# mLSTM stage of a two-layer streaming encoder: scores and the keys' transposes in one matmul per head, values transposed ahead of them

## The reference

```
def step(carry, xs):
    C, n, m = carry
    qc, kc, vc, ic, fc = xs
    b = jnp.cumsum(fc, axis=-1)
    D = b[..., :, None] - b[..., None, :] + ic[..., None, :]
    D = jnp.where(causal, D, NEG)
    inter = b + m[..., None]
    mt = jnp.maximum(inter, jnp.max(D, axis=-1))
    S = jnp.einsum('bhtd,bhsd->bhts', qc, kc) * jnp.exp(D - mt[..., None])
    w_inter = jnp.exp(inter - mt)
    num = jnp.einsum('bhts,bhsd->bhtd', S, vc) + w_inter[..., None] * jnp.einsum('bhvk,bhtk->bhtv', C, qc)
    den = jnp.sum(S, axis=-1) + w_inter * jnp.einsum('bhk,bhtk->bht', n, qc)
    h = num / jnp.maximum(jnp.abs(den), jnp.exp(-mt))[..., None]
    mL = mt[..., -1]
    ws = jnp.exp(b[..., -1:] - b + ic - mL[..., None])
    decay = jnp.exp(b[..., -1] + m - mL)
    C_new = decay[..., None, None] * C + jnp.einsum('bhs,bhsv,bhsk->bhvk', ws, vc, kc)
```

## Time and profile before

| | us |
|---|---|
| median of three timed runs | 1317.18 |
| lowest, highest | 1316.38, 1317.22 |
| the profiled execution, its own time | 1317.47 |
| its span, first to last instruction | 1315.7 |
| TensorE busy | 1296.2 |
| VectorE busy | 897.3 |
| ScalarE busy | 611.2 |
| mLSTM stage of layer 0, own keys of pair 0 to own keys of pair 3 | 29.10 |

### The profile page before, as it was taken

One profiled execution on the slowest core, in us unless ns is written; L12 is line 12 of the kernel. 1 busy time (PEld: TensorE's weight loads), 2 busy tenths in 40 slices (PEclk: granted clock), 3 DMA queues, 4 the chain that ended last, 5 costly groups with the idle time before them and its releaser, 6 DMA issues.

```text
span 1315.7 us, 24594 instructions
## 1 busy us (share of the span) xinstructions
PE 1296.2 (99%) x9943; PEld 1264.8 (96%) x9943; DVE 897.3 (68%) x1504; ACT 611.2 (46%) x1134; POOL 62.6 (5%) x43
## 2 busy tenths in 40 slices
PE   7999999999999999999999999999999999999998
PEld 6999899999999999999999998999999999999997
DVE  7776787798586475586666768878965846846734
ACT  6324335488256155165242333456852732822833
POOL 0000001000000000000610000000000000000032
PEclk9999999999999999999999999999999999999999
DMA  7322220223232232222252222212322322322312
GB/s 220 82 71 66 64 65 33 81 72 121 65 97 97 66 94 96 90 69 96 84 123 71 65 65 65 65 33 81 97 97 65 97 97 65 114 77 74 119 65 73
DMA packets 115630, 109.74 MB, mean 83 GB/s; under 512 B 18830, under 2 KB 109398, under 8 KB 115542
## 3 DMA queue, kind: packets, MB, share of 16 engines
q1 hardware_dynamic: 110256, 104.54, 26.3%
q10 hardware_dynamic: 5286, 3.97, 1.0%
HBM read 104.69 MB, written 3.81 MB: 82 GB/s over the span
## 4 chain that ended last, share of the span: by engine, by line
PE 89%; DVE 6%; ACT 3%; issue 1%; DMA 0%; SPq 0%; ACTq 0%; DVEq 0%
PE psum L1717 56%; PE psum L2039 8%; PE psum L2041 8%; PE psum L2040 8%; PE psum L1770 1%; PE psum L1859 1%; PE psum L1955 1%; PE psum L1947 1%; PE psum L1920 1%; PE psum L1936 1%; PE psum L1964 1%; ACT w_hi L545 1%; PE psum L1892 1%; PE psum L1888 1%; PE psum L1877 0%
## 5 line engine op out<-in xcount | busy, mean ns | idle before, releaser
L1717 PE MATMUL psum<-hid_h,w_hi 128*128 128x288 f32 x1232 | 266.6, 297 | 0.0
L1717 PE MATMUL psum<-hid_l,w_hi 128*128 128x288 f32 x1232 | 263.8, 295 | 0.0
L1717 PE MATMUL psum<-hid_h,w_lo 128*128 128x288 f32 x1232 | 263.7, 295 | 0.0
L1717 PEld LDWEIGHTS psum<-hid_h,w_hi 128*128 128x128 f32 x1232 | 197.3, 188 | 1.1 <-issue 0.3
L1717 PEld LDWEIGHTS psum<-hid_h,w_lo 128*128 128x128 f32 x1232 | 197.6, 188 | 0.0
L1717 PEld LDWEIGHTS psum<-hid_l,w_hi 128*128 128x128 f32 x1232 | 197.4, 188 | 0.0
L1717 PE MATMUL psum<-xh,w_hi 128*128 128x288 f32 x800 | 178.9, 305 | 2.8 <-ACT x L590 1.9
L1602 DVE TENSOR_TENSOR tmp<-psum,rms 128x576 f32<-128x576 f32 x63 | 47.7, 758 | 185.9 <-PE psum L1717 185.8
L1717 PE MATMUL psum<-xh,w_lo 128*128 128x288 f32 x800 | 172.1, 296 | 0.0
L1717 PE MATMUL psum<-xl,w_hi 128*128 128x288 f32 x800 | 172.0, 296 | 0.0
L803 ACT ACTIVATE w_hi<-stage 128x1024 fp32r<-128x1024 f32 x64 | 67.7, 1058 | 219.0 <-PE psum L1717 218.2
(11 more groups left out here) (331 smaller groups left out, 2546.8 us busy)
## 6 DMA issues: line engine op xcount, KB each, us to landing
stage<-in_w_up SPq DMA_DIRECT2D x32, 1024.0 KB, 5.6
stage<-in_w_down SPq DMA_DIRECT2D x32, 1024.0 KB, 5.1
stage<-in_w_in SPq DMA_DIRECT2D x18, 1024.0 KB, 5.2
stage<-in_w_in SPq DMA_DIRECT2D x16, 256.0 KB, 4.4
stage<-in_w_out SPq DMA_DIRECT2D x8, 512.0 KB, 6.9
stage<-in_w_out SPq DMA_DIRECT2D x4, 1024.0 KB, 5.7
z<-in_x_prompt SPq DMA_DIRECT2D x4, 512.0 KB, 5.6
out<-z SPq DMA_DIRECT2D x3, 512.0 KB, 2.7
```

The lines of the kernel that those rows point to most:

```text
L1717: ins = M(acc[t % 2][:, a, :], lhs(w), mov[:, k, a * HALF:(a + 1) * HALF], start=first and n == 0, stop=last and n == 2)
```

## The change

The keys are the stationary side of the scores' product already (`z[:, h, cs]`). The change makes the moving side 256 columns wide: the identity and the queries, in two blocks of 128. The identity's block gives the keys' transpose, the queries' block the scores. So that one access pattern reaches both, `z` gets 128 columns ahead of its first tile, which GpSimd fills with the identity once. The results of heads 0 and 1 go to bank 4 and those of heads 2 and 3 to bank 7; the values' transposes go to bank 6 and stand ahead of the scores. The units are dealt out anew. The short pair's merged product also moves 256 columns, of which 64 queries are used.

```diff
-M_FILL = ((2, 1, 1, 1), (2, 2, 1, 1), (2, 2, 1, 1), (2, 2, 1, 1), (2, 1, 0, 0))
+M_FILL = ((1, 1, 3), (2, 1, 3), (2, 1, 3), (2, 1, 3), (2, 1, 0))
...
-        z = place("z", [P, 4 * MH, T])
+        z_all = place("z", [P, P + 4 * MH * T])
+        z = z_all[:, P:].rearrange("p (n t) -> p n t", n=4 * MH)
...
+            pool.wait_ge(s_const, 16)
+            nc.gpsimd.tensor_copy(z_all[:, 0:P], ident).then_inc(s_idc, 1)
             pool.wait_ge(s_rcon, 1)
...
                 def values(p):
                     r = rows(p)
                     act.wait_ge(s_tv, NP * l + p + 1)
-                    A(vtok[0:r, :, 0:MD], psum[0:r, 7, :].rearrange("p (h d) -> p h d", h=MH), ACT.Copy).then_inc(s_vev, 1)
+                    A(vtok[0:r, :, 0:MD], psum[0:r, 6, :].rearrange("p (h d) -> p h d", h=MH), ACT.Copy).then_inc(s_vev, 1)
...
                     r = rows(p)
-                    act.wait_ge(s_tk, NP * l + p + 1)
+                    act.wait_ge(s_sw, NP * l + p + 1)
                     act.wait_ge(s_gtd, l + 1)
                     for h in range(MH):
-                        ins = A(ktok[0:r, h], psum[0:r, 7, h * MD:(h + 1) * MD], ACT.Copy, scale=gT[0:r, p, 0, h:h + 1])
+                        keys_out = psum[0:r, (4, 7)[h // 2], h % 2 * 256:h % 2 * 256 + P]
+                        ins = A(ktok[0:r, h], keys_out, ACT.Copy, scale=gT[0:r, p, 0, h:h + 1])
                     ins.then_inc(s_kev, 1)
...
                     fill("m", p, 0)
-                    head_squares(p)
                     if p < NP - 1:
                         values(p + 1)
+                    head_squares(p)
                     fill("m", p, 1)
...
-                    V.tensor_tensor(sw[0:r, :, 0:r], ch(4, p)[0:r], eexp[0:r, :, 0:r], ALU.mult).then_inc(s_sw, 1)
+                    pairs = lambda buf: buf[0:r].rearrange("p (k h) t -> p k h t", k=2)[:, :, :, 0:r]
+                    scores = psum[0:r, 4:8:3, :].rearrange("p k (h b t) -> p k h b t", h=2, b=2)[:, :, :, 1, 0:r]
+                    V.tensor_tensor(pairs(sw), scores, pairs(eexp), ALU.mult).then_inc(s_sw, 1)
...
                     r, cs = rows(p), pair_cols(p)
                     if p:
                         pe.wait_ge(s_st, NP * l + p)
+                        pe.wait_ge(s_hx, MH * (NP * l + p))
                     for h in range(MH):
-                        ins = M(psum[0:r, 4, head(p, h)], z[:, h, cs], z[:, 4 + h, cs], start=True, stop=True)
+                        at = P + (4 + h) * T + p * P
+                        ident_and_query = z_all[:, 0:2 * at].rearrange("p (b c) -> p b c", b=2)[:, :, 0:P]
+                        out = psum[0:r, (4, 7)[h // 2], h % 2 * 256:(h % 2 + 1) * 256].rearrange("p (b c) -> p b c", b=2)
+                        ins = M(out, z[:, h, cs], ident_and_query, start=True, stop=True)
                     ins.then_inc(s_swp, 1)
...
-                        ins = TR(psum[0:r, 7, h * MD:(h + 1) * MD], z[:, tile + h, pair_cols(p)], ident)
-                    ins.then_inc(signal, 1)
+                        ins = TR(psum[0:r, 6, h * MD:(h + 1) * MD], z[:, 8 + h, pair_cols(p)], ident)
+                    ins.then_inc(s_tv, 1)
...
                 scores(0)
                 exponents(0)
-                token_major(0, 0, s_tk)
                 fill(l, "a", NC, 0)
                 fill(l, "p", 0, 0)
-                pe.wait_ge(s_kev, NP * l + 1)
+                pe.wait_ge(s_ao, NC * (l + 1))
                 pe.wait_ge(s_evac, TILES * l + S_WOA)
-                token_major(0, 8, s_tv)
+                values(0)
                 fill(l, "p", 0, 1)
-                pe.wait_ge(s_ao, NC * (l + 1))
...
                     if p:
                         from_state(p)
+                    if p < NP - 1:
+                        if p:
+                            pe.wait_ge(s_ownc, (NP - 1) * l + p)
+                        else:
+                            pe.wait_ge(s_hx, MH * (a + 1))
+                        values(p + 1)
                     fill(l, "m", p, 1)
                     if p < NP - 1:
                         scores(p + 1)
-                        pe.wait_ge(s_hx, MH * (a + 1))
-                        token_major(p + 1, 8, s_tv)
                         exponents(p + 1)
                     fill(l, "m", p, 2)
-                    if p < NP - 1:
-                        pe.wait_ge(s_vev, a + 2)
-                        token_major(p + 1, 0, s_tk)
-                    fill(l, "m", p, 3)
```

More of the change, by code:

```diff
@@ L269, in hymba_step @@
         s_aoh, s_ao = sem("s_aoh"), sem("s_ao")
-        s_tv, s_vev, s_tk, s_kev = sem("s_tv"), sem("s_vev"), sem("s_tk"), sem("s_kev")
+        s_tv, s_vev, s_kev = sem("s_tv"), sem("s_vev"), sem("s_kev")
         s_e, s_ex, s_swp, s_sw = sem("s_e"), sem("s_ex"), sem("s_swp"), sem("s_sw")
@@ L277, in hymba_step @@
         s_zclear = sem("s_zclear")
+        s_idc = sem("s_idc")
         s_ncr, s_bd = sem("s_ncr"), sem("s_bd")
@@ L771, in _ @@
                     fill("m", p, 2)
-                    fill("m", p, 3)
                 fill("m", NP, 0)
@@ L1439, in _ @@
                 fill("m", NP - 1, 2)
-                fill("m", NP - 1, 3)
                 fill("m", NP, 0, late=False)
@@ L1931, in exponents, with values @@
                     M(e5, acl[:, p * P:(p + 1) * P], bd[:, a % 2, :, 0:r], start=False, stop=True).then_inc(s_e, 1)
-                def token_major(p, tile, signal):
+                def values(p):
                     r = rows(p)
                     for h in range(MH):
-                        ins = TR(psum[0:r, 7, h * MD:(h + 1) * MD], z[:, tile + h, pair_cols(p)], ident)
-                    ins.then_inc(signal, 1)
+                        ins = TR(psum[0:r, 6, h * MD:(h + 1) * MD], z[:, 8 + h, pair_cols(p)], ident)
+                    ins.then_inc(s_tv, 1)
                 part = lambda r, bank, n: psum[0:r, bank, n * (MD + 1):(n + 1) * (MD + 1)]
@@ L1977, in _ @@
                 pe.wait_ge(s_rcon, 1)
+                pe.wait_ge(s_idc, 1)
                 scores(0)
                 exponents(0)
-                token_major(0, 0, s_tk)
                 fill(l, "a", NC, 0)
                 fill(l, "p", 0, 0)
-                pe.wait_ge(s_kev, NP * l + 1)
+                pe.wait_ge(s_ao, NC * (l + 1))
                 pe.wait_ge(s_evac, TILES * l + S_WOA)
-                token_major(0, 8, s_tv)
+                values(0)
                 fill(l, "p", 0, 1)
-                pe.wait_ge(s_ao, NC * (l + 1))
                 for p in range(NP):
```

## The result

The changed kernel takes 1325.8 us (median of four runs, 1325.34 to 1325.98) beside 1317.2 us of the kernel before (four runs, 1316.38 to 1317.41): the ratio is 1.0065, interval 1.0050 to 1.0081. It is slower by 8.5 us; the forecast of 1323.4 us had +6.2, and the range 1319.0 to 1326.0 holds the time by 0.2 us. The profiled execution's own time is 1325.96 us, its span 1324.2 us, against 1317.47 us and 1315.7 us before.

What follows compares the result with a forecast made beforehand. TensorE, busy for 1296.2 of 1315.7 us, was taken as the bound. The terms 3.0 + 1.3 + 2.2 + 1.5 - 1.2 - 0.6 = +6.2 us gave a median of 1323.4 us, range of 8 in 10 1319.0 to 1326.0 us.

Steps and rivals of the forecast that it cites:

- The bound and the clock: Whole kernel: added TensorE work adds time, its clock stays at 2.4 GHz, and nothing behind the stage swallows the loss.
- The price of 256 fp32 columns: Merged product on TensorE: 214 ns an instruction, 1.71 us for eight, from the 288-column row; low end 145 ns.
- free columns: Rival: 256 columns hide under the weight load at 110 ns an instruction, waits stay; 1315.2 us, chance 0.06.
- half-width price: Rival: merged instructions cost 145 ns, as the attention's products with half the array's columns; +0.7 us, 1317.9 us, chance 0.06.
- The merged product as a whole: Merged products replacing scores and keys' transposes on TensorE: +3.0 us in 128-row pairs, +1.3 us in short pairs.
- The wait for the values: TensorE ahead of the values of pair 1, on VectorE's copy: 1.1 us once a layer, +2.2 us.
- The scores' waits: TensorE ahead of the scores, on VectorE's combination: 0.25 us for three scores a layer, +1.5 us; could be nil.
- The gap of pair 1: Pair 1's 0.9 us over pair 2, from late VectorE, shrinks to 0.25: -0.6 us a layer, -1.2 us.
- The gap of the short pair: The short pair's own-keys product no longer starts late after VectorE's weighted scores: -0.3 us a layer, -0.6 us.
- The keys on ScalarE: ScalarE's keys wait for VectorE's weighted scores instead of the transposes: no cost, some 0.3 us of slack stay.
- the rival of late keys: Rival: ScalarE's keys end after the state product is due, eight later pairs lose about 0.4 us each; 1326.6 us, chance 0.06.
- The rival without waits: Rival: the new waits don't appear, only products and closed gaps count; +2.5 us, 1319.7 us, chance 0.09.

Runs made afterwards that it cites:

- product apart, GpSimd behind the heads: Changed kernel with separate 128-column scores' products and keys' transposes, and GpSimd's multiplication waiting for VectorE's heads' combination: 1319.77 us.
- product apart, GpSimd as it was: Changed kernel with separate 128-column scores' products (64 in the short pair), then four keys' transposes; order, banks and waits kept: 1321.04 us.
- The run with 192 columns: Changed kernel with 96 instead of 128 columns in each of the merged product's two blocks, so results differ: 1321.87 us, one run.
- GpSimd moved: Changed kernel with GpSimd's multiplication for the exponents' rows waiting for VectorE's four heads' combinations instead of the own-keys product: 1324.25 us.
- second unit in pair 0: Changed kernel with one unit of pair 0 moved from behind the exponents to ahead of the values of pair 1: 1324.67 us.

## Why the prediction was right, and where its size was off

The ledger, from run to run:

| step | measured, us | forecast, us |
|---|---|---|
| before -> product apart, GpSimd behind the heads (1319.8) | +2.5 | |
| -> product apart, GpSimd as it was (1321.0) | +1.3 | |
| the new order, both together | +3.8 | +1.9 (2.2 + 1.5 - 1.2 - 0.6) |
| -> merged product (1325.8) | +4.8 | +4.3 (3.0 + 1.3) |
| sum | +8.5 | +6.2 |

Step by step:

- **The bound and the clock: right.** TensorE is the engine that ends the chain, the granted clock is 1.00 in every window, and no stretch outside the mLSTM stages changed by what can be seen (8.6 us of the stages against 8.5 us in all). Nothing behind the stage swallowed the loss.
- **The price of 256 fp32 columns: right.** 217 ns against 214, taken from the row with 288 columns and not from the half-width row with 145 ns. The run with 192 columns shows the law: 0.83 ns a column, once that is more than the load's 110 ns. This decides against the rivals of free columns (1315.2) and of the half-width price (1317.9). By the Trainium skill (TensorE: Matmul & The Clock Gate, Back-to-back issue gap), N moving columns take N/2.4 + 2.5 ns; at 256 that is 109 ns, and the trace has 217. The measurement decides: for fp32 the rule is off by a factor of two here.
- **The merged product as a whole: 0.5 us short.** 3 ns more in each of the 64 instructions of the long pairs are 0.2 us; in the short pair it took 1.86 us (2.18 from its first instruction to the first unit, less 0.32 for its exponents), where 1.71 was forecast, 0.3 us in two layers.
- **The wait for the values: right in place and size.** Start at 3.67 us, forecast 3.66; pair 0 at 9.47, forecast 9.5. What the prediction did not see is that TensorE's idle time there is not what is lost: filling it with a unit gave nothing once GpSimd was moved, for the values still come behind VectorE's copy, and what hangs on them over ScalarE and VectorE comes no earlier. That this is one chain fits the runs; no run shortened one of its links on VectorE or ScalarE in pair 0, but one lengthened one, in the kernel before: a gate piece 0.85 us longer made pair 0 0.74 us longer.
- **The scores' waits: right.** 0.31 us in three places a layer, forecast 0.25.
- **The gap of pair 1: the step that failed.** "The waits and the longer product give it 1.5 us more before pair 1, while the work queued on it is the same", so 0.65 of the 0.9 us were to go. The forecast for the pair was 11.0 us; 11.79 were measured, and in layer 1 11.76. Those are 1.5 us of the 2.3 by which the sum was short, and some 1.3 of them are the gap, which stayed as it was. Two things were overlooked. The work queued on VectorE is the same, but it waits for ScalarE's rounding, and that was made to wait for the late scores through the keys: 0.95 of the 1.49 us went there. The prediction looked at this queue in pair 2 only and called the rounding "needed many units later"; for TensorE that holds, but VectorE takes `w_lo` in order, ahead of the new state. And GpSimd's multiplication, which lay 0.49 us over `w_lo` in the trace of before, moved onto it for 1.0 us. The row of before had said so: 1.57 us there beside 1.22 elsewhere. The second is tested: with GpSimd moved the gap closes. The first is read from the order and the rows, and was not tested by itself. The range held because its upper end had allowed for both gaps staying open; one did, and the time came within 0.2 us of that end.
- **The gap of the short pair: nearly right.** From the last step of the units to the own-keys product it was 0.29 us and is 0.09 now. The whole stretch took 0.88 us more, forecast 0.6: the longer product (0.15), the scores' wait (0.06) and this (0.09) make the difference.
- **The keys on ScalarE: no cost in pairs 2 and 3, as forecast.** TensorE never waits for `ktok` in them, and the rival of late keys (1326.6) is ruled out by its mechanism, though its time is near the measured one. In pair 1 the keys do set when the weight tile is rounded, see above.
- **The rival without waits (1319.7) is out:** both waits are in the trace.

## What to carry to other kernels

Merging two products so that one weight load serves both pays only as long as the load is the longer part; with fp32 and 128-row weights load and columns were already in balance at 128 columns, so the second 128 cost about twice the transposes that they replaced (0.85 us a pair for 0.44). When work is moved on an engine that is the bound, follow every queue that its result passes, to the end: a wait filled in one place came back in another, since the chain over two other engines was the longer one. And a gap is only closed if the work that caused it does not move along with it; look at what runs beside it on GpSimd in the old trace.

## What the hardware showed that I had not expected

VectorE and GpSimd hold each other up in some of their instructions, by nearly the whole of the overlap. GpSimd's multiplication takes 1.28 us; VectorE's `w_lo`, with both inputs and the output in SBUF, takes 1.22 us alone:

| kernel, pair 1 | GpSimd, from start to end | `w_lo` from | overlap with GpSimd's rest, us | `w_lo`, us |
|---|---|---|---|---|
| GpSimd moved | not beside it | 210.80 | 0 | 1.23 |
| second unit in pair 0 | 209.92 to 211.20 | 210.77 | 0.43 | 1.51 |
| before | 209.40 to 210.69 | 210.20 | 0.49 | 1.57 |
| changed kernel | 211.24 to 212.52 | 211.51 | 1.01 | 2.09 |

The surplus over 1.22 us is the overlap less 0.14 us in all three. Layer 1 shows the same lengths, 1.57 us before and 2.09 us in the changed kernel. The gate's TENSOR_SCALAR, 0.23 us alone, took 1.08 us with 0.99 us of GpSimd's work still to come. Each time VectorE ends as if it had begun 0.14 us before GpSimd ended, and GpSimd keeps its 1.28 us. The kernel with GpSimd behind the heads shows the other order too. Its timeline, pair 1, behind the product from the state:

```profile
215.45 0.68 DVE L1414 TENSOR_TENSOR hid_l<-tmp,hid_h 128x512 fp32r<-128x512 f32 x1
215.61 1.65 POOL L505 TENSOR_TENSOR bd<-ncr,rconst 128x512 fp32r<-128x512 f32 x1 [10.73 <-DVE hx L1383]
216.05 1.23 DVE L1391 SCALAR_TENSOR_TENSOR small<-hx 128x4 f32<-128x4 f32 x1
```

Here VectorE came first, kept its 0.68 us, and GpSimd took 1.65 us, 0.37 more. The next VectorE instruction, on four columns and 0.16 us long elsewhere, then ran until GpSimd ended. TensorE did not wait for it there, which is why the move still paid. Not all of VectorE is held up: in pair 0 of the same kernel a RECIPROCAL ran wholly beside GpSimd in its usual 1.05 us.

```profile
203.60 1.28 POOL L505 TENSOR_TENSOR bd<-ncr,rconst 128x512 fp32r<-128x512 f32 x1 [68.78 <-DVE hx L1376]
203.70 1.05 DVE L1271 RECIPROCAL z<-z 128x144 f32<-128x144 f32 x1
```

This fits the Trainium skill (SBUF — State Buffer, Who interferes with whom): VectorE and GpSimd share a pair of ports under an exclusive lock that the first to start holds for its whole instruction, and it is wanted by a VectorE instruction with two inputs in SBUF when GpSimd's reads SBUF, or by one in a mode that uses both ports. The traces agree for both orders, with 0.87 us of surplus for two inputs and 0.85 us for the TENSOR_SCALAR; that the TENSOR_SCALAR ran in such a mode no trace shows.
